# The second layer's projection with key and query units interleaved, heads turned back two units later, and the first tile's eviction and product ahead of the second tile

## The reference

```
for i in range(2):
    h  = modulate(rmsnorm(x,   norm1_g[i]), sh1,  sc1)     # 1024 rows
    hc = modulate(rmsnorm(ctx, norm1_g[i]), sh1c, sc1c)    #  256 rows
    y, yc = attention_i(h, hc, wqkv, ...)                  # layer 1: no yc
    x = x + g1 * y ;  ctx = ctx + g1c * yc
    out = moe(modulate(rmsnorm(x | ctx, norm2_g[i]), sh2, sc2))
    x = x + g2 * out[:1024] ;  ctx = ctx + g2c * out[1024:]
```

```
qkv = u @ wqkv                       # [rows, 1024] @ [1024, 1536]
q = rmsnorm(heads(qkv[:, :1024]), q_g)      # 16 heads of 64, image rows only
k = rmsnorm(heads(qkv[:, 1024:1280]), k_g)  #  4 heads of 64, all rows
v = qkv[:, 1280:]                           #  4 heads of 64, all rows
q, k = rope(q), rope(k)                     # image rows
```

## Time and profile before

| | us |
|---|---|
| time, median of 3 runs | 3026.74 |
| lowest and highest of them | 3025.78, 3032.27 |
| the profiled execution, its own time | 3040.78 |
| its span, first to last instruction | 3039.0 |
| the second layer's projection, first transpose to the last product's end | 1751.03 to 1975.67 |

### The profile page before, as it was taken

The page is one execution under the profiler, slowest core; times in us unless marked ns, Lnnn a source line. Parts: engine busy times, 40 slices in busy tenths (PEclk is TensorE's granted clock), DMA queues, the critical chain, the costliest instruction groups (busy, mean ns, idle before and its releaser), DMA issues.

```text
span 3039.0 us, 38516 instructions
## 1 busy us (share of the span) xinstructions
PE 2742.1 (90%) x15193; PEld 1495.6 (49%) x15193; DVE 1295.9 (43%) x2395; ACT 764.7 (25%) x1707; POOL 652.4 (21%) x895
## 2 busy tenths in 40 slices
PE   6999999999999987999999779979999779987973
PEld 2444433898986543333333234468875433422321
DVE  3544301899995553111111254479974521110113
ACT  2211100677774100000000152156651000000001
POOL 2555300455553211000000044500002100000000
PEclk9999999999999987999999989989999789998997
DMA  6344467424242228999999675253322298999997
GB/s 253 112 101 138 162 241 245 104 53 105 53 108 84 104 76 365 381 387 396 426 381 426 250 273 131 70 125 57 70 70 99 100 404 367 384 396 425 393 390 301
DMA packets 199412, 684.33 MB, mean 225 GB/s; under 512 B 26688, under 2 KB 122096, under 8 KB 166208
## 3 DMA queue, kind: packets, MB, share of 16 engines
q1 hardware_dynamic: 101344, 583.01, 51.6%
q10 hardware_dynamic: 84896, 61.07, 6.4%
q0 software_dynamic: 12992, 37.77, 3.2%
HBM read 607.81 MB, written 83.43 MB: 227 GB/s over the span
## 4 chain that ended last, share of the span: by engine, by line
PE 76%; DMA 14%; DVE 6%; issue 1%; ACT 1%; SPq 1%; POOL 1%; ACTq 0%; POOLq 0%; DVEq 0%
PE psum L446 18%; PE psum L1794 14%; DMA moe_ring<-in_e_w 11%; PE psum L1350 8%; PE psum L1809 8%; PE psum L1011 5%; PE psum L960 5%; PE psum L1149 3%; PE psum L1136 3%; PE psum L965 2%; PE psum L1177 2%; PE psum L413 1%; PE psum L1771 1%; PE psum L1339 1%; PE psum L1975 1%
## 5 line engine op out<-in xcount | busy, mean ns | idle before, releaser
L1794 PE MATMUL psum<-moe_ring,moe_xT 128*32 128x512 f32 (+2 forms) x3744 | 616.4, 623 | 57.9 <-DMA moe_ring<-in_e_w 55.7
L446 PE MATMUL psum<-qkv_w,act_hT 128*128 128x512 f32 x1376 | 612.7, 599 | 1.4 <-ACT act_hT L547 1.3
L1794 PEld LDWEIGHTS psum<-moe_ring,moe_xT 128*32 128x32 f32 (+2 forms) x3744 | 207.5, 126 | 435.9 <-issue 433.1
L446 PEld LDWEIGHTS psum<-qkv_w,act_hT 128*128 128x128 f32 x1376 | 257.5, 192 | 308.9 <-issue 306.4
L1809 PE MATMUL psum<-moe_ring,moe_hT 128*32 128x512 f32 (+2 forms) x1872 | 302.7, 606 | 15.9 <-DMA moe_ring<-in_e_w 15.1
L1878 DVE TENSOR_TENSOR moe_hh<-psum,moe_sg 128x512 f32<-128x512 f32 x42 | 29.0, 691 | 634.6 <-PE psum L1794 634.6
L1350 PE MATMUL psum<-wo,out_oT 128*128 128x512 f32 x576 | 256.6, 601 | 1.9 <-DVEq L1397 1.5
L1846 ACT ACTIVATE moe_sg<-psum 128x512 f32<-128x512 f32 x42 | 25.1, 597 | 777.1 <-PE psum L1794 777.1
L1076 DVE TENSOR_REDUCE att_nmax<-psum 128x1 f32<-128x1280 f32 x144 | 201.8, 1402 | 26.2 <-PE psum L960 24.2
L960 PE MATMUL psum<-att_kT,att_q 128*128 128x512 f32 (+1 forms) x832 | 195.5, 370 | 9.7 <-ACTq L174 5.1
L1028 ACT ACTIVATE att_prob<-psum,att_nmax 128x1280 f32<-128x1280 f32 (+1 forms) x160 | 184.9, 1159 | 48.5 <-DVE att_nmax L1076 45.8
(11 more groups left out here) (249 smaller groups left out, 3286.8 us busy)
## 6 DMA issues: line engine op xcount, KB each, us to landing
moe_ring<-in_e_w SPq DMA_DIRECT2D x192, 2048.0 KB, 20.1
ada_w<-in_ada_w SPq DMA_DIRECT2D x48, 1024.0 KB, 6.6
qk_d<-qkv_stg ACTq DMA_DIRECT2D x112, 256.0 KB, 2.8
att_q<-qk_d SPq DMA_DIRECT2D x32, 640.0 KB, 12.0
att_q<-qk_d SPq DMA_DIRECT2D x64, 256.0 KB, 5.2
qkv_w<-in_a_wqkv SPq DMA_DIRECT2D x6, 2048.0 KB, 9.8
att_kT<-qk_d SPq DMA_DIRECT2D x32, 320.0 KB, 5.8
prep_y<-y_d SPq DMA_DIRECT2D x10, 1024.0 KB, 7.1
```

Source lines behind the costliest of these rows:

```text
L446: ins = nc.tensor.matmul(psum[:, u.par, :], hT[:, k, u.t * P:(u.t + 1) * P], qw[:, u.C % 2, k], start=(k == 0), stop=(k == KD - 1))
L1794: ins = nc.tensor.matmul(psum[part, bank, :], xT[:, 4 * half + k, part], ring[:, CHUNK[l][r, half] % RING, k, bank * DE:(bank + 1) * DE], ...
```

## The change

In the second layer the tiles are taken in the order 0, 1, 8, 2, 9, 3, 4, 5, 6, 7, and an image tile's kv unit is followed at once by its first q unit (chunk 1); the context tiles have a kv unit alone. The eight units of chunk 2 follow as before. Tile work (`turn`, `put`, `norm`, `combine` and so on) is tied to the round of a tile's first unit, by the table `STARTS`. `BACK` sets how many units later the heads are turned back: 1 in the first layer as before, 2 in the second. `evac` and its stores become two functions, and the stores go out one round later than the eviction, in both layers. Chunk 1 is loaded behind tile position 2 instead of 4. Ahead of the second layer's loop, `norm(0)` comes before `combine(1)`, `put(0)` before `square(1)`, and PE multiplies unit 0 before `turn(1)`.

```diff
+    TILE_ORDER = [list(range(TA)), [0, 1, TX, 2, TX + 1, 3, 4, 5, 6, 7]]
+        order = [(chunk, t) for chunk, section in enumerate(sections) for t in range(section[3])]
+        if l:
+            order = [(chunk, t) for t in TILE_ORDER[l] for chunk in range(2) if t < TX or chunk == 0] + [(2, t) for t in range(TX)]
+    BACK = [1, 2]
+    STARTS = [{min(u.n for u in UNIT[l] if u.t == t): pos for pos, t in enumerate(TILE_ORDER[l])} for l in range(2)]
...
# SP, second layer
-            if t == 4:
+            if t == 2:
                 load_qkv(sp, l, 1)
...
-            sp.wait_ge(s_qst[par], 16 + 32 * 25)
+            sp.wait_ge(s_qst[par], 48 + 32 * max(u.R // 2 for u in UNIT[1] if u.kind == "kv" and u.par == par))
         sp_att1_keys(sp)
-        sp.wait_ge(s_qst[0], 16 + 32 * 26)
...
# PE
         for u in units:
             s = u.n
-            if s + 1 < TA:
-                turn(s + 1)
+            first = l == 1 and s == 0
+            if not first and STARTS[l].get(s, TA) + 1 < TA:
+                turn(STARTS[l][s] + 1)
             product(u)
-            if s:
-                turn_back(units[s - 1])
+            if first:
+                turn(1)
+            if s >= BACK[l]:
+                turn_back(units[s - BACK[l]])
...
# ACT
+        def store(u):
+            if not u.heads:
+                return
+            nb = u.heads // 2
             act.wait_ge(s_qev, u.R + 3)
             for part in range(2):
                 act.dma_start(qk_d[...], qstg[:, u.par, part, 0:nb].bitcast(F32)).then_inc(s_qst[u.par], 16)
...
             weigh(0)
+            square(0)
             weigh(1)
-            square(0)
+            act.wait_ge(s_cold, 2)
+            put(0)
+            square(1)
             weigh(2)
-            square(1)
-            act.wait_ge(s_cold, 2)
...
+        back = BACK[l] + 1
+        for s in range(len(units) + back + 1):
+            pos = STARTS[l].get(s)
+            if pos is not None:
+                if l == 0 or pos:
+                    put(pos)
+                if pos + 2 < TA:
+                    square(pos + 2)
+                if l and pos + 3 < TA:
+                    weigh(pos + 3)
             if 1 <= s <= len(units):
                 take(units[s - 1])
-            if s >= 2:
-                evac(units[s - 2])
+            if s > back:
+                store(units[s - back - 1])
+            if back <= s < len(units) + back:
+                evac(units[s - back])
...
# DVE
             combine(0)
+            norm(0)
             combine(1)
-            norm(0)
+            norm(1)
             combine(2)
-            norm(1)
...
             if 1 <= s <= len(units):
                 mean(units[s - 1])
-            if l and s + 3 < TA:
-                combine(s + 3)
-            if s >= 2:
-                low(units[s - 2])
+            if l and pos + 3 < TA:
+                combine(pos + 3)
+            if s > BACK[l]:
+                low(units[s - 1 - BACK[l]])
             if 1 <= s <= len(units):
                 rotate(units[s - 1])
```

More of the change, by code:

```diff
@@ L294, in __init__ @@
             self.n, self.chunk, self.t, self.kind, self.heads, self.which, self.part = n, chunk, t, kind, heads, which, part
+            self.pos = TILE_ORDER[l].index(t)
+            self.first = self.last = False
             self.U = n + 60 * l
@@ L306, in build @@
                                   [("kv", 4, 1, TA), ("qk", 8, 0, TX), ("qk", 8, 0, TX)]]):
-        for chunk, (kind, heads, which, nt) in enumerate(sections):
-            for t in range(nt):
-                UNIT[l].append(Unit(l, len(UNIT[l]), chunk, t, kind, heads, which, part_of(l, chunk)))
+        order = [(chunk, t) for chunk, section in enumerate(sections) for t in range(section[3])]
+        if l:
+            order = [(chunk, t) for t in TILE_ORDER[l] for chunk in range(2) if t < TX or chunk == 0] + [(2, t) for t in range(TX)]
+        for chunk, t in order:
+            kind, heads, which, nt = sections[chunk]
+            UNIT[l].append(Unit(l, len(UNIT[l]), chunk, t, kind, heads, which, part_of(l, chunk)))
+        for chunk in range(len(sections)):
+            mine = [u for u in UNIT[l] if u.chunk == chunk]
+            mine[0].first = mine[-1].last = True
+    BACK = [1, 2]
+    STARTS = [{min(u.n for u in UNIT[l] if u.t == t): pos for pos, t in enumerate(TILE_ORDER[l])} for l in range(2)]
     FIRST_V = 40
@@ L327, in load_x @@
                 sp.wait_ge(s_pu, t - 1)
[L328 removed]
+            tile = TILE_ORDER[l][t]
+            sp.dma_start(pxt1[:, t % 2], xs_d[tile * P:(tile + 1) * P, :]).then_inc(s_px[t % 2], 16)
         else:
@@ L447, in product @@
             ins.then_inc(s_qacc, 1)
-            if u.n + 1 == len(units) or units[u.n + 1].chunk != u.chunk:
+            if u.last:
                 pe.wait_ge(s_qacc, u.U + 1)
@@ L486, in pe_front @@
                     pe_columns(pe, 1)
-        turn_back(units[-1])
+        for u in units[-BACK[l]:]:
+            turn_back(u)
     def act_small_loads(act, step):
@@ L531, in weigh @@
                 act.wait_ge(s_pst[t % 2], 16 * (t // 2))
-            nc.scalar.activation(pu[:, t % 2], py2[:, t % 2, 0], ACT.Copy, scale=wsel[:, 0, t:t + 1]).then_inc(s_py0, 1)
+            tile = TILE_ORDER[l][t]
+            nc.scalar.activation(pu[:, t % 2], py2[:, t % 2, 0], ACT.Copy, scale=wsel[:, 0, tile:tile + 1]).then_inc(s_py0, 1)
         def square(t):
@@ L652, in pool_front @@
         for s in range(len(units) + 1):
-            if s + 2 < TA:
-                root(s + 2)
+            if STARTS[l].get(s, TA) + 2 < TA:
+                root(STARTS[l][s] + 2)
             if s:
@@ L784, in dve_front @@
             combine(0)
+            norm(0)
             combine(1)
-            norm(0)
+            norm(1)
             combine(2)
-            norm(1)
-        for s in range(len(units) + 2):
-            if s < TA:
-                if l == 0:
-                    put(s)
-                if s + 2 < TA:
-                    norm(s + 2)
+        for s in range(len(units) + 1 + BACK[l]):
+            pos = STARTS[l].get(s, TA)
+            if pos < TA and l == 0:
+                put(pos)
+            if pos + 2 < TA:
+                norm(pos + 2)
             if 1 <= s <= len(units):
                 mean(units[s - 1])
-            if l and s + 3 < TA:
-                combine(s + 3)
-            if s >= 2:
-                low(units[s - 2])
+            if l and pos + 3 < TA:
+                combine(pos + 3)
+            if s > BACK[l]:
+                low(units[s - 1 - BACK[l]])
             if 1 <= s <= len(units):
```

28 lines of the change are left out of this document (13 added, 15 removed).

## The result

| | before | changed |
|---|---|---|
| median of 4 runs, us | 3029.14 | 3011.05 |
| lowest and highest | 3025.78, 3032.27 | 3008.3, 3013.78 |
| span of the profiled execution | 3039.0 | 3012.0 |

The ratio is 0.9943 with a 95% interval of 0.9929 to 0.9957: 17 us faster (13 to 22), where 14.2 were forecast. (More runs of before were made for the result, so its median is not the 3026.74 of the prediction.)

A forecast was written before the change was run, and what follows sets the result against it. PE was taken to bound the kernel, losing time in the second layer's projection to a loop between ACT and DVE. From 3026.74 us, -15.9 + 1.6 - 6.4 + 1.0 + 0.2 + 5.3 = -14.2 gave 3012.5, range 3004 to 3022.

The forecast's parts named there:

- tile stage, slow clock included: Second layer's ten tiles: all 15.9 us lost in hindered rounds come back, less 1.6 of remaining slow clock.
- front: Ahead of the second layer's tiles: first product 8.2 us earlier, less 0.9 slow clock and 0.9 for turn(1): -6.4 us.
- chunk 2: Second layer, ahead of unit 18: its chunk can load only after kv unit 16, a wait of +1.0 us (0 to 1.8).
- turn-backs and tail: Second layer's end: one turn-back moved behind the last product (-0.5), one more store pair before the last eviction (+0.7): +0.2 us.
- first layer's stores: First layer, behind the fifth chunk's load: an eviction waits for stores to land and PE stalls, +5.3 us (0 to 7.1).
- the tightest places: Second layer's tile stage: the bank a product needs back, about 2 us spare, less than 1 at the first tiles.
- behind the burst: First layer, fifth chunk: the reading that stores land with the loads' end, at 289.6, costing 7.1 us.
- No stall in the first layer: Rival: the first layer's eviction does not stall PE, giving 3007.2 us; chance 0.19.
- The second unit waits for its bank: Rival, second layer: scaling comes 1 us late at each of eight image tiles, giving 3020.5 us; chance 0.17.
- signs of being right: First product 8 us earlier, no PE gaps over 0.5 (products 1–17), first-layer eviction waiting 6, last product 20 nearer first transpose.
- The loop holds: Rival, second layer: each of ten tiles' chains still keeps PE waiting 3.1 us, giving 3043, slower; chance 0.07.
- nothing arrives: Rival: projection ends earlier but the attention begins no sooner, its first query rows or keys late: 3027 us; chance 0.06.

The follow-up runs named there:

- e1: Changed kernel with the first layer's stores again issued directly behind their eviction: ratio to before 0.9948, first layer's stretch 488.7 us (changed: 488.7).
- e7: Changed kernel with the second layer's units back in chunk order, all else kept: second layer's projection stage 242.0 us, ratio to before 0.9953.
- e12: Changed kernel with second-layer stores joined to their eviction and BACK = 1, interleaving and new front kept: projection stage 251.4 us, ratio to before 0.9985.
- e11: Changed kernel with second-layer units in chunk order and BACK = 1, later stores and new front kept: projection stage 245.6 us, ratio to before 0.9970.
- e5: Kernel before with only the front of the second layer's projection changed: projection stage 257.1 us (before: 258.1), ratio to before 0.9996.
- e6: Changed kernel with the second layer's front put back as before: projection stage 242.4 us (changed: 239.8), ratio to before 0.9961.
- e2: Changed kernel with the first layer's stores still a round late but issued behind the eviction: first layer's stretch 498.6 us (changed: 488.7), ratio to before 0.9976.
- e3: Changed kernel with second-layer stores issued directly behind their eviction, units interleaved, BACK = 2: projection stage 245.9 us, ratio to before 0.9967.
- e10: Changed kernel with second-layer units in chunk order and stores joined to their eviction, BACK = 2, new front: projection stage 253.5 us, ratio to before 0.9999.
- e9: Changed kernel with DVE's scaling ahead of combine, plus constant multiplications on PE in the second layer's idle lead: projection stage 237.6 us, ratio to before 0.9950.

## Why the prediction was right, and where it was not

The total was met: -14.2 us forecast, -17 measured (-13 to -22). That 3012.5 came as near to 3011.05 as it did is in part luck, since the median of before stood 2.4 us higher in the result's runs; and the terms were off by more than the total: the stores by 4.8 us one way, tile stage and front by 1.4 and 1.0 the other.

| term | predicted | in the trace |
|---|---|---|
| tile stage, slow clock included | -14.3 | -12.9 |
| front | -6.4 | -5.4 |
| chunk 2 | +1.0 | +0.8 |
| turn-backs and tail | +0.2 | 0.0 |
| first layer's stores | +5.3 | +0.5 |
| sum | -14.2 | -17.0 |

The terms inside S1 make -17.5 of its -18.3; the rest I cannot assign. The split between the first two is a matter of place in one profile: in e1, whose second layer is the changed one, product 0 takes 8.9 us instead of 10.1, product 2 waits 3.0 us instead of 1.6 and takes 8.8, and both start product 2 at 44.0 us into the stage.

*Tile stage.* All 15.9 us of hindered rounds went, as the step said, and 3.0 came back: product 2 follows its turn after 2.65 us instead of 0.87, product 3 its turn-back after 1.44 instead of 0.22. Both were named as the tightest places. The 1.6 us that I had left for slow clock did not come as such (granted clock 1.00 between products 1 and 17). The first wait is late rows: the expert outputs of the fourth tile in order are now issued behind chunk 1's 2 MB, and took 13.9 us (8.4 before the change).

```profile
prep_y<-y_d SPq DMA_DIRECT2D x1, 1024.0 KB, 13.9
...
1762.86 1.15 ACT L549 ACTIVATE prep_u<-prep_y,wsel 128x1024 f32<-128x1024 f32 x1 [5.24 <-DMA prep_y<-y_d]
...
1767.83 0.41 DVE L770 TENSOR_REDUCE qkv_ms<-qkv_sq 128x4 f32<-128x256 f32 x1
...
1769.73 0.43 DVE L785 TENSOR_TENSOR qkv_xn<-psum,qkv_rs 128x256 f32<-128x256 f32 x1 [1.49 <-POOL qkv_rs L653]
...
1775.31 2.59 POOL L653 TENSOR_TENSOR qkv_rs<-qkv_ms,neghalf 128x8 f32<-128x8 f32 x1
```

ACT waited 5.2 us for them, combine followed, and only then mean and scaling of unit 0. The second wait is POOL's root for 8 heads, 2.59 us beside combine (1.67 in the first layer, where nothing is combined). On this the Trainium skill ("SBUF — State Buffer", "SBUF: two separate sides") had it right in direction and about right in price: the root ended 0.3 us behind the combine and the gap was 1.2 us. What I had made of the rule, that all of POOL's work waits for the end of the combine, the rows contradict: combine is three instructions, the rule is about single ones, and the root started inside it. Roots of 2.60 us stand beside later combines too (at 1789.0, 1812.1 and 1835.3), and no product waits there.

The *reason* I gave first for the tile stage was wrong. I wrote that two units per tile cover the loop; chunk order without the interleaving is within 2.2 us of the changed kernel (e7), and the interleaving alone recovers 5.7 of 17.3 (e12). What pays most in chunk order is the part I put second: ACT's `put` no longer stands behind a wait for `low`. There, later stores take 11.5 us off, with either BACK (e11, e7), and turning back later 3.6. Once the units are interleaved it is the other way round: later stores take 2.6 or 6.1, turning back later 5.5 or 9.0. The interleaving itself is worth 5.7 or 7.6 with joined stores, 2.2 in the whole change. With later stores but BACK = 1 it is even worse than chunk order (248.8 against 245.6): PE waits 4.8 us at the first tiles, three times 1.2 behind combine and 2.9 at a store that lands late, in chunk order 3.8 and 1.6 at the first tiles and 1.4 at such a store.

*Front.* The start moved by 7.9 us (8.2 predicted), the slow clock cost 1.6 (0.9), turn(1) 0.9. The prediction's 2.3 us of slow stretch rested on no row; the trace has 3.1. But this term is not the front's own: alone it is worth 1.0 (e5), beside the rest 2.6 (e6). The starts of front and tile stage hang together: put the front back and the waits of 3.0 us ahead of products 2 and 3 go with it (e6), so that the 5.4 gained by place and the 3.0 lost by place are one term of 2.6. The sum came out because each had been counted with the other in place.

*First layer.* This step failed: 0.5 us for 5.3, and in S0 nothing to be seen (488.7 with the later stores, 488.7 without). I had taken the stores' time of issue as the end of `take` (273.3 in the old trace); they are not held by it and leave with its start, ahead of the chunk's load and of the three that follow. The end "0, if the earlier stores slip through ahead of the loads" is nearly what happened: they were through as the chunk's load ended, before most of the conditioning's packets moved. That the stall itself is no invention is shown by e2. Of my two readings of a landing, "behind the burst" is the one that held: stores issued 0.85 us behind the chunk's load landed at 288.2, 16 us later, as the last of the loads ended (287.9). The Trainium skill ("DMA: Bandwidth & Descriptors", "Queues, rings and completion order") has each DMA engine go round the queues packet by packet, and so it does here: 302 packets of the one queue to 302 of the other. Wrong was what I made of it. A store did not share from its issue on but from 3.9 us later, and a turn each is no equal share when one side's packets are up to 16 times as large; so a microsecond of issue cost eight of landing.

*Rivals and signs.* No stall in the first layer: so it was, nearly. The second unit waits for its bank: at two units instead of eight. So two of the signs of being right did not come: the eviction that waits 6 us with PE's gap of 5 behind it, and PE without gaps over 0.5 us between products 1 and 17; and the last product came 17 us nearer to the first transpose, not 20. The loop holds, and nothing arrives: neither; the attention's first multiplication follows the last product by 13.5 us, 13.1 before.

## What to carry over

When an engine's round in an in-order loop waits for a result of the same round, look first for that wait and move its consumer one round back: the two moves of this kind (the stores, 6.1 us in the whole change, and the turn-back, 9.0) were worth more than the reordering of the products (2.2). Shares of a gain measured by taking parts away one at a time do not add, since what one part frees the next wait takes up. And a transfer's place in the queues can be worth many times its own issue time, so the issue order around a large load deserves a look of its own.

## What was not expected of the hardware

- A store of 2 x 256 KB issued 0.08 us ahead of a 2 MB load and three 1 MB loads had landed by 280.1 (under 9 us), one issued 0.85 us behind the load only at 288.2 (16 us), with the same loads: its first packet moved 3.9 us after the issue instead of 1.0, and then packets of 512 bytes took turns with packets of up to 8 KB.
- Idle gaps of 2.3 to 2.9 us on PE are at times followed by a product of 8.8 us in place of 7.1 (e3 at 1774.27 and 1802.17), at times not (e10 at 1806.87). A gap so costs up to 1.7 us beyond its length.
- PE multiplied constants for 9.2 us, idled 3.9, and its next transposes still ran at the full clock (e9: 1.09 us for eight at a granted clock of 1.00; 1.94 in the changed kernel after 18.7 us of idling).
